# A four-stage transformer kernel on one core: residual, LayerNorm, down and output projections laid out by tokens instead of by channels

## The reference, cut to what matters

```python
h = _layernorm(ALPHA * h + mix, ln_mix_g[i], ln_mix_b[i])
h = _layernorm(ALPHA * h + _swiglu(h, ffn_w_gu[i], ffn_w_down[i]), ln_ffn_g[i], ln_ffn_b[i])
```

## Time and profile before

| | |
|---|---|
| median of 3 runs | 2604.16 us |
| profiled execution, its own time | 2603.37 us |
| its span | 2601.5 us |
| PE busy | 2448.5 us (94%) |
| DVE busy | 988.9 us (38%) |
| ACT busy | 686.0 us (26%) |
| POOL busy | 1183.7 us (45%) |
| HBM read | 199.81 MB, 78 GB/s over the span |

### The profile page before, as it was taken

One profiled execution on the slowest core, in us unless ns is written; L12 is line 12 of the kernel. 1 busy time (PEld: TensorE's weight loads), 2 busy tenths in 40 slices (PEclk: granted clock), 3 DMA queues, 4 the chain that ended last, 5 costly groups with the idle time before them and its releaser, 6 DMA issues.

```text
span 2601.5 us, 27614 instructions
## 1 busy us (share of the span) xinstructions
PE 2448.5 (94%) x10718; PEld 1939.6 (75%) x10718; DVE 988.9 (38%) x1659; ACT 686.0 (26%) x841; POOL 1183.7 (45%) x441
## 2 busy tenths in 40 slices
PE   8999999999999799999999999999977779999998
PEld 6657788887777678888877788888754448788887
DVE  6665200006556550000383600001797765200006
ACT  2221421221322232212222222122233331421221
POOL 4221654453423345535546356355444652555451
PEclk9999999998999899999999999999998878999998
DMA  4100232232211112322212132222120100232230
GB/s 173 66 30 36 81 113 87 91 113 73 73 49 51 46 49 97 114 80 101 93 65 101 52 108 107 89 88 106 57 97 25 41 17 33 81 113 82 96 108 38
DMA packets 27442, 203.05 MB, mean 78 GB/s; under 512 B 3040, under 2 KB 4192, under 8 KB 6752
## 3 DMA queue, kind: packets, MB, share of 16 engines
q1 hardware_dynamic: 27360, 201.92, 21.6%
HBM read 199.81 MB, written 2.10 MB: 78 GB/s over the span
## 4 chain that ended last, share of the span: by engine, by line
PE 77%; DVE 16%; POOL 3%; ACT 3%; issue 2%; DMA 0%; DVEq 0%; ACTq 0%; SPq 0%
PE bank L814 21%; PE bank L818 21%; PE bank L819 21%; DVE fY L1672 2%; DVE sqt L1293 2%; PE bank L903 2%; PE bank L860 2%; PE bank L1008 2%; POOL XL L657 1%; POOL wlo L624 1%; PE bank L941 1%; PE bank L850 1%; PE bank L988 1%; DVE X L1362 1%; PE bank L910 1%
## 5 line engine op out<-in xcount | busy, mean ns | idle before, releaser
L624 POOL TENSOR_TENSOR wlo<-raw,whi 128x2048 fp32r<-128x2048 f32 (+3 forms) x156 | 820.5, 5260 | 475.6 <-ACT whi L348 475.5
L814 PE MATMUL bank<-XH,whi 128*128 128x512 f32 x1972 | 784.5, 398 | 21.0 <-DVE fz L1658 8.0
L818 PE MATMUL bank<-XL,whi 128*128 128x512 f32 x1972 | 773.8, 392 | 0.0
L819 PE MATMUL bank<-XH,wlo 128*128 128x512 f32 x1972 | 773.6, 392 | 0.0
L348 ACT CAST whi<-raw 128x2048 fp32r<-128x2048 f32 (+3 forms) x156 | 336.6, 2158 | 497.3 <-PE bank L814 497.3
L814 PEld LDWEIGHTS bank<-XH,whi 128*128 128x128 f32 x1972 | 374.1, 190 | 125.6 <-issue 29.4
L819 PEld LDWEIGHTS bank<-XH,wlo 128*128 128x128 f32 x1972 | 373.9, 190 | 79.5
L818 PEld LDWEIGHTS bank<-XL,whi 128*128 128x128 f32 x1972 | 374.5, 190 | 76.1 <-issue 0.7
L1377 DVE TENSOR_TENSOR hf<-sil,bank 128x512 f32<-128x512 f32 x88 | 60.6, 688 | 870.9 <-PE bank L819 855.2
L641 POOL TENSOR_TENSOR HL<-hf,HH 128x512 f32 (+1 forms) x88 | 114.4, 1300 | 380.3 <-ACT HH L392 380.3
L814 PE MATMUL bank<-HH,whi 128*128 128x512 f32 x704 | 275.9, 392 | 0.7 <-POOL wlo L624 0.7
(11 more groups left out here) (238 smaller groups left out, 2459.7 us busy)
## 6 DMA issues: line engine op xcount, KB each, us to landing
raw<-w_ffn_gu SPq DMA_DIRECT2D x88, 1024.0 KB, 4.7
raw<-w_ffn_d SPq DMA_DIRECT2D x16, 1536.0 KB, 6.5
raw<-w_ffn_d SPq DMA_DIRECT2D x16, 1280.0 KB, 5.5
raw<-w_diff_in SPq DMA_DIRECT2D x8, 1536.0 KB, 6.5
raw<-w_ev_in SPq DMA_DIRECT2D x6, 1024.0 KB, 4.7
raw<-w_od_in SPq DMA_DIRECT2D x4, 1536.0 KB, 6.4
raw<-w_mla_pair SPq DMA_DIRECT2D x4, 1280.0 KB, 5.7
raw<-w_od_glu SPq DMA_DIRECT2D x4, 1024.0 KB, 4.7
```

The costliest lines, as they stand in the source:

```text
L624: pool.tensor_tensor(wlo[s][:, 0:size], raw[s][:, 0:size], whi[s][:, 0:size].bitcast(F32), ALU.subtract).then_inc(lo_ready, 1)
L814: ins = pe.matmul(out, whi[s][:, off:off + P], xh, start=start, stop=False)
L818: pe.matmul(out, whi[s][:, off:off + P], xl, start=False, stop=False)
L819: return pe.matmul(out, wlo[s][:, off:off + P], xh, start=False, stop=stop)
```

## The change

Activations that are carried from layer to layer lie with tokens on the partitions: X is [128, 4, 1024], block t holding tokens 128t to 128t+127. The output projections and the down projections turn the operands round: the activation's 128 x 128 block is stationary, and 512 columns of the weights (one half d of the output channels) are the moving operand (`token_product`). The number of these matmuls stays the same. Half d=0 is accumulated in four banks, one per token block, k in the outer loop (`first_steps`). For half d=1 the last two weight units are held together, and PE finishes one token block after the other (`last_units` with `pair`), transposing the normalised block t-1 back to channels behind the products of block t (`token_transposes`).

The LayerNorm is DVE's: `add_half`, BN_STATS, BN_AGGR, then two scalar_tensor_tensor per half with gain and bias from GB, a [128, 2048] tile with the rows repeated over the partitions, which SP loads anew for each norm (1 MB). POOL takes the root of four columns of one value per norm. ACT copies the transposed halves from PSUM to XH, DVE subtracts to XL (`low_half`). Column sums, spreads, keep-warm matmuls and first means go for these eight norms; the one over 512 channels in "od" stays.

The two slots for weights become a ring of 6144 columns: units of 2048 columns have three places, those of 3072 two. The output projections have four units of 2048. In the last heads a step of the output projection is now 12 matmuls. The opening makes all its XH products first, then those with XL. All loops are written out. In the differential stage the opening has two units of 1536.

```diff
+DOWN = ((4, 4, 4), (2, 4, 4))
...
+            def load_norm(norm):
+                if norm:
+                    sp.wait_ge(xn_ready, 8 * norm)
+                if norm == 6:
+                    sp.wait_ge(tap_added, 2 * (TAPS - 1))
+                sp.dma_start(GB[:], gb[norm]).then_inc(gb_in, 16)
...
+            def layer_norm(banks):
+                for t in range(NB):
+                    for d in range(2):
+                        act.wait_ge(xt_done, halves.at(1))
+                        act.copy(XH[:, 4 * d:4 * d + 4, t * P:(t + 1) * P],
+                                 bank[banks[(2 * t + d) % 4]][:].rearrange("p (k q) -> p k q", q=P)).then_inc(xh_ready, 1)
+                        halves.add()
...
+            def layer_norm():
+                for t in range(NB):
+                    norms.add()
+                    pool.wait_ge(tvar_ready, norms.at())
+                    pool.tensor_tensor(troot[:, t:t + 1], tvar[:, t:t + 1], neg_half[:, 0:1], ALU.pow).then_inc(troot_ready, 1)
...
+            def opening(nt, ks=range(KD)):
+                off = begin_unit() - ks[0] * nt * P
+                def lhs(wt, k, t):
+                    return wt[:, off + (k * nt + t) * P:off + (k * nt + t + 1) * P]
+                for k in ks:
+                    if k % 4 == 0:
+                        pe.wait_ge(xh_ready, norms.at(k // 4 - 1))
+                            if k == 0 and which is whi:
+                                claim(t)
+                            release(pe.matmul(bank[t][:], lhs(which, k, t), XH[:, k, :], start=k == 0 and which is whi, stop=False))
+                for k in ks:
+                    if k % 4 == 0:
+                        pe.wait_ge(xl_ready, norms.at(k // 4 - 1))
+                    for t in range(nt):
+                        ins = pe.matmul(bank[t][:], lhs(whi, k, t), XL[:, k, :], start=False, stop=k == KD - 1)
+                        if k == KD - 1:
+                            tile_end(ins, t)
...
-            def first_mean():
...
+            def token_product(b, t, off, xh, xl, start, stop):
+                rows = slice(t * P, (t + 1) * P)
+                release(pe.matmul(bank[b][:], xh[:, rows], whi[:, off:off + HALF], start=start, stop=False))
+                pe.matmul(bank[b][:], xl[:, rows], whi[:, off:off + HALF], start=False, stop=False)
+                ins = pe.matmul(bank[b][:], xh[:, rows], wlo[:, off:off + HALF], start=False, stop=stop)
+                if stop:
+                    ins.then_inc(acc_done, 1)
+                    accs.add()
+                    freed[b] = (acc_free, accs.n)
...
+            def first_steps(off, ks, source, first, depth, b0):
+                for k in ks:
+                    xh, xl = source(k)
+                    pe.wait_ge(act_lo, los.at(k + 1))
+                    for t in range(NB):
+                        if k == 0:
+                            claim(b0 + t)
+                        token_product(b0 + t, t, off + (k - first) * HALF, xh, xl, k == 0, k == depth - 1)
+            def last_units(units, source, depth, b0, pair):
+                if not pair:
+                    for ks in units:
+                        off = begin_unit()
+                        for t in range(NB):
+                            if ks[0] == 0:
+                                claim(b0 + t)
+                            for k in ks:
+                                token_product(b0 + t, t, off + (k - ks[0]) * HALF, *source(k), k == 0, k == depth - 1)
+                    return
+                for ks in units[:-2]:
+                    off = begin_unit()
+                    for t in range(NB):
+                        if ks[0] == 0:
+                            claim(b0 + t)
+                        for k in ks:
+                            token_product(b0 + t, t, off + (k - ks[0]) * HALF, *source(k), k == 0, False)
+                offs = [begin_unit()]
+                for t in range(NB):
+                    for i, ks in enumerate(units[-2:]):
+                        if t == 0 and i == 1:
+                            offs.append(begin_unit(0))
+                        if ks[0] == 0:
+                            claim(b0 + t)
+                        for k in ks:
+                            token_product(b0 + t, t, offs[i] + (k - ks[0]) * HALF, *source(k), k == 0, k == depth - 1)
+                    if t > 0:
+                        token_transposes(t - 1)
+                used_up[0] += 1
+                token_transposes(NB - 1)
+                norms.add(2 * NB)
+            tb0 = [0]
+            def token_transposes(t):
+                if norms.n == 14 * NB:
+                    return
+                for d in range(2):
+                    b = tb0[0] + (2 * t + d) % 4
+                    pe.wait_ge(xn_ready, norms.at(2 * t + d + 1))
+                    claim(b)
+                    for c in range(4):
+                        k = 4 * d + c
+                        ins = pe.transpose(bank[b][:, c * P:(c + 1) * P], X[:, t, k * P:(k + 1) * P], ident)
+                    ins.then_inc(xt_done, 1)
+                    freed[b] = (xl_ready, norms.at(2 * t + d + 1))
...
+            def out_units(source=attended):
+                los.add(KD)
+                tb0[0] = 0
+                last_units(OUT_KS, source, KD, 4, True)
...
-                    def down_unit(j, wait_x=False):
-                        s = begin_unit()
-                        for t in range(2):
-                            tile(s, 2 * j + t, [(k * 2 + t) * P for k in range(n)], HH, HL, wait_x=wait_x and t == 0)
-                    for u in range(4):
-                        down_unit(u % 2, u == 0)
-                        if half == 1 and u == 1:
-                            first_mean()
+                    for j in range(n):
+                        if half == 0 and j == 0:
+                            opening(2)
+                        else:
+                            unit_tiles(2, 2 * (j % 2))
+                    ends = list(itertools.accumulate(DOWN[half], initial=0))
+                    groups = [range(a, b) for a, b in zip(ends, ends[1:])]
+                    for ks in groups:
+                        first_steps(begin_unit(), ks, hidden, ks[0], n, 4)
                     los.add(n)
...
+                    tb0[0] = 4
+                    last_units(groups, hidden, n, 0, half == 1)
...
-            def residual(scale):
...
+            def add_half(t, d, b, scale):
+                x = xhalf(t, d)
+                dve.wait_ge(acc_done, accs.at(1))
+                if scale == 1.0:
+                    ins = dve.tensor_tensor(x, x, bank[b][:], ALU.add)
+                else:
+                    ins = dve.scalar_tensor_tensor(x, x, scale, bank[b][:], ALU.mult, ALU.add)
+                ins.then_inc(acc_free, 1)
+                accs.add()
+            def half_stats(t, d):
+                dve.wait_ge(acc_free, accs.at())
+                link(dve.bn_stats(stats[:, t, d, :], xhalf(t, d)))
+            def low_half(t, d, banks):
+                dve.wait_ge(xh_ready, 8 * norms.n + 2 * t + d + 1)
+                cols = slice(t * P, (t + 1) * P)
+                dve.tensor_tensor(XL[:, 4 * d:4 * d + 4, cols], bank[banks[(2 * t + d) % 4]][:].rearrange("p (k q) -> p k q", q=P),
+                                  XH[:, 4 * d:4 * d + 4, cols].bitcast(F32), ALU.subtract).then_inc(xl_ready, 1)
+            def token_norm(b0, tbanks, scale):
+                split = norms.n < 7
+                for t in range(NB):
+                    add_half(t, 0, tbanks[t], scale)
+                    half_stats(t, 0)
+                for t in range(NB):
+                    add_half(t, 1, b0 + t, scale)
+                    half_stats(t, 1)
+                    link(dve.bn_aggr(moment[:, t, :], stats[:, t, :, :]))
+                    dve.tensor_scalar(tvar[:, t:t + 1], moment[:, t, 1:2], LN_EPS, None, ALU.add).then_inc(tvar_ready, 1)
+                    if split and t in (1, 2):
+                        for d in range(2):
+                            low_half(t - 1, d, tbanks)
+                    if t == 0:
+                        dve.wait_ge(gb_in, 16 * (norms.n + 1))
+                    for d in range(2):
+                        dve.scalar_tensor_tensor(xhalf(t, d), xhalf(t, d), moment[:, t, 0:1], GB[:, d * HALF:(d + 1) * HALF],
+                                                 ALU.subtract, ALU.mult).then_inc(step, 1)
+                        steps.add()
+                    dve.wait_ge(troot_ready, 4 * norms.n + t + 1)
+                    for d in range(2):
+                        dve.wait_ge(step, steps.at(d - 1))
+                        dve.scalar_tensor_tensor(xhalf(t, d), xhalf(t, d), troot[:, t:t + 1], GB[:, D + d * HALF:D + (d + 1) * HALF],
+                                                 ALU.mult, ALU.add).then_inc(xn_ready, 1)
+                for t in (2, 3) if split else ():
+                    for d in range(2):
```

(58 more changed lines are left out.)

834 lines of the change are left out of this document (331 added, 503 removed).

## The result

The changed kernel takes 2482.56 us (median of 4 runs, 2480.32 to 2486.0) against 2604.11: ratio 0.9535, 95% interval 0.9523 to 0.9547, so 121.6 us less. Forecast was 2513, 91 us less. The profiled execution has 2481.4 us.

What follows compares the result with a forecast made beforehand. PE was taken as the bound, busy 94% of the span. 2603.4 - 172.4 (norms and first means) + 84.4 (new norm costs) - 3 (other moves) = 2512.4, with 0.8 2513 us; range 2480 to 2559.

Steps and rivals of the forecast that it cites:

- The bound and what goes: PE bounds the kernel; eight norms' cost of 165.4 us and 7.0 us of first means go, together 172.4 us.
- rival D: Turned products run slower, 0.032 us more for each of 2880; at 0.26 us the time is 2608; chance 0.03.
- (a): Transposes of token blocks 0 and 1 between products of the last pair: 1.8 us on the path per norm.
- (b): The tail, from the last product of block 3 to the start of the next opening: 6.5 us per norm.
- I charge it in full: In the tail, POOL's root of 1.03 us counted in series with DVE's centring pair, 5.0 us instead of 4.0.
- (c): After the tail's idle gap the opening's first matmuls run at a lower clock: 1.6 us per norm, at least 0.
- Rival C: Without warming matmuls the clock stays low through each opening, 28.8 us per norm: 2723 us in all; chance 0.03.
- (d): In the pair DVE needs 5.9 us per block, 0.6 over with the root in series: 1.0 us per norm.
- What else moves: Outside the norms, mainly output projection steps in the last heads, between -10.2 and +3 us: taken as -3.
- The ring loads two units ahead, so nothing: Weight ring, some 20 us of PE work ahead, covers the loads of GB and X: no cost.
- Written-out loops: nothing: Loops cost nothing where only products run, so writing them out wins nothing.
- rival A: Norm tighter: root beside centring, clock holds, DVE keeps up, last heads cover all 10.2 us: 2480 us; chance 0.16.

Runs made afterwards that it cites:

- experiment 4: The changed kernel, but DVE waits for POOL's root before it centres each block: 2493.12 us, 10 us slower.
- Experiment 9: The changed kernel with 13 fp32 warming matmuls ahead of the last block's transposes in seven norms: 2473.35 us, 9 to 10 us faster.
- experiment 6: The changed kernel, but in od's GLU part ACT rounds a unit only once PE has begun the unit before, as with two slots: 2491.34 us.
- experiment 8: The changed kernel with POOL's split of a unit in four instructions in the attention stages and their output projections: 2465.96 us, 17 to 18 us faster.
- Experiment 1: The changed kernel, but last-head steps with k above 0 leave out token block 3, 9 matmuls instead of 12: 2481.7 us, ratio 0.9542 to the kernel before.
- experiment 5: The changed kernel with every BN_STATS made twice: 2493.57 us, 8 us slower.
- experiment 12: The kernel before the change, with POOL's low part of every unit in four instructions: 2583.05 us, 22 us faster than before.

## Why the prediction was right, and where its sizes were off

The mechanism is the forecast's, but its sizes gave some 30 us too little gain. The time lies only 2.6 us above the lower end of the range (2480), less than the changed kernel's own runs spread over (5.7 us), so that it lies inside is in part luck.

**The bound and what goes**: right. The feed-forward stages are 1536 matmuls in 348.16 us without transposes, 0.2267 each, and turned products keep the pace (rival D refuted). The 165.4 us and the first means are gone.

**(a) Transposes**: 1.8 forecast, 1.82 measured.

**(b) The tail**: 6.5 forecast, 5.63 measured (5.69 behind od). The failed step is "I charge it in full", POOL's root in series. It lies beside the centring; experiment 4, which makes the series, adds 0.75. The mean of 1225 ns of L1362 misled me: 28 of its 32 instructions take 0.69 us and four take 4.97, each begun just behind a POOL split of 2048 columns (L624, 4.8 us). They say what such a split costs DVE, and nothing of a root of one column, which the centring pair doesn't wait for; here it is the root that takes longer, 0.98 instead of 0.54. The other terms hold: half 0 of the block is ready 4.1 us behind the product (4.0 forecast without the root), and 1.5 more to the opening (1.5). In seven norms that is 6.1 us, and the end is 7.1 behind the last product instead of 8.1.

**(c) The clock**: 11.2 us forecast, 9.7 measured behind the start of the openings in the profiled execution. Of this 0.5 behind ffn0 is no clock (0.4 is a wait for dVT); the rest is 0.2 to 1.7 per norm. Experiment 9 shows the mechanism: the same idle stretch filled, and the opening starts at full pace. The granted clock (third number from the end) shows the difference between two openings behind equal tails with equal waits (3.05 and 3.06 us), that behind mla and that behind diff:

```profile
250.46:253.94 3.48, 3.48 (x8) 2.79 (x9) 1.46 (x3) 3.03 (x3) 0.65 (x1) 0.51 0.02 5
901.60:905.00 3.40, 3.40 (x15) 2.69 (x16) 1.46 (x3) 3.25 (x3) 0.86 (x1) 1.00 0.02 5
```

The clock fell behind six of the seven tails and not behind diff's; the spared norm is ffn0's in experiment 6 and ffn1's in 8, and where the clock fell before the last transposes (experiments 1, 5, 6, 8) the tail is up to 0.46 longer. So 1 to 2 us per norm is a matter of the execution, and what decides it is open. Rival C is refuted, and so are the 11 us of extra loss that would have followed from the Trainium skill's rule on transposes if the whole tail were idle for the clock. Whether transposes count as work for it is still open: no run had transposes alone for so long.

**(d) DVE late in the pair**: 7 us forecast, 0 measured. I took 5.9 us per block, and 0.6 over with the root. It is 5.6: BN_AGGR and the variance 0.32 instead of 0.4, the two XL 1.19 instead of 1.4, from start to start. Experiments 4 and 5, each with 0.7 more per block, still leave the feed-forward stages as they are; only the pairs of three mixers in 5 show a wait, of 0.6 to 0.7 us.

Sum of (a) to (d) and the end: 84.4 forecast, 69.0 measured.

**What else moves**: the weakest step, -3 us where the stages gave 18.9. By part (transposes and first mean taken out):
- The last heads: od -1.8, diff +0.1, MLA -3.0, together -4.7 against my -3. In kernels that leave them alone diff's and od's last heads differ by about 2 us between executions, so this term held as far as can be told. Experiment 1 shows that in MLA's last pair the added work is mostly paid, so cover is not what made that pair 3.0 shorter; the smaller splits may be (experiment 12 shortens it by 4.1, 68.9 to 64.7, with pieces alone), which was not tried here alone.
- "The ring loads two units ahead, so nothing": wrong in od's GLU part, -4.3. There a unit is short (24 or 48 matmuls, 5 to 11 us of PE) and ACT's and POOL's splits, which had to wait until PE had begun the unit before, were late. Experiment 6 gives it all back; experiment 12 gains the same 4.3 without a third place, so the term that I had wrong is that the splits are in time, and either change mends it.
- Od's first three heads, -3.0 (137.4 to 139.4 us in kernels that leave them alone, against 140.4): the output projection's unit is 2048 columns instead of 3072, so DVE stands 4.6 instead of 7.1 us beside its split. I had the earlier trace rows for this in the last differential head and did not look for the same pair elsewhere. Experiments 8 and 12 show the mechanism, not this amount alone.
- "Written-out loops: nothing": wrong by a little. A feed-forward layer is 0.5 us shorter (349.52 less 0.87 for the mean, against 348.16), 1.5 in the last; the differential opening's 2.41 us have shrunk to 0.54, and the stage has won 4.2 before its last head. That the loops are the cause was not tried alone. Nor was the rest, ev -1.1 and MLA ahead of its last pair +1.4.
- GB: it takes 7.1 us from issue to landing instead of the 4.7 taken, and nobody waits for it. Held.

Total: 15.4 too much at the norms, 15.9 too little elsewhere, 2513 - 31 = 2482. The truth lay almost at rival A (2480), but not for its reasons alone: of its four conditions the root beside the centring and DVE keeping up came true, the clock did not hold, and the last heads did not cover all 10.2 us (in MLA's pair most of the work is paid).

## What to carry to other kernels

Put the LayerNorm where its statistics fall within a partition, and let each block's norm run under the next block's products: the order alone was worth 51 of 122 us. When an engine pair shares a port, look for every place where the waiting one's duration equals the other's instruction, and cut that instruction: 22 us in the kernel before, for five lines, though its differential heads lost 4 us by it. When the idle stretch ahead of an opening can't be removed, fill it exactly: 13 matmuls won 9 us, 30 lost 16 to 18.

## What the runs showed of the hardware that I had not expected

- One fp32 matmul of 128 x 128 takes 0.22 us, as two rows of the trace; the transposes, of the same shape, take 0.11.
- POOL's split in four pieces takes 6.3 us beside DVE instead of 4.6, and the whole kernel is still 17 us faster.
- The loss of clock behind the same tail of 5.63 us differs from norm to norm, 0.2 to 1.7 us, in one and the same execution, with a granted clock of 1.00 over the opening's start in one and 0.51 in another; with 2.9 us of the tail filled it is 0.1 to 0.3.
- The root of one column takes 0.54 us beside a DVE operation that reads PSUM (L1383) and 0.98 beside one whose operands are both in SBUF (L1403).
